# Two of eight Toeplitz blocks' vectors made inside attention, with a block load, a table load and an addition moved

## The reference, cut to what matters

```python
for layer in range(DEPTH):                     # DEPTH = 2
    if layer % 2 == 0:                         # layer 0: attention over the last 128 positions, with sinks
        mp, kp_new, vp_new = swa_prompt(rmsnorm(xp, norm_mix[layer]), *attn)
        ms, ks_new, vs_new = swa_sample(rmsnorm(xs, norm_mix[layer]), cache_k[a], cache_v[a], *attn)
    else:                                      # layer 1: h_l = A h_(l-1) + B u_l, y = Re(C h) + D u
        mp, rp_new, ip_new = s5_mix(rmsnorm(xp, norm_mix[layer]), h0, h0, *ssm)
        ms, rs_new, is_new = s5_mix(rmsnorm(xs, norm_mix[layer]), state_re, state_im, *ssm)
    xp = xp + mp
    xs = xs + ms
    xp = xp + hier_moe(rmsnorm(xp, norm_ffn[layer]), *moe_w)
    xs = xs + hier_moe(rmsnorm(xs, norm_ffn[layer]), *moe_w)
y_prompt, y_sample = rmsnorm(xp, norm_final), rmsnorm(xs, norm_final)

# what the SSM's constants are (s5_mix)
abar = exp(delta * (a_re + 1j * a_im))         # one complex number per group and state
bbar = (abar - 1) / a * b                      # "B-bar"; its factor (abar - 1) / a is CF in the kernel
```

## Time and profile before

| | us |
|---|---|
| median of three runs | 926.05 |
| lowest, highest | 925.84, 927.51 |
| the profiled execution's own time | 925.76 |
| its span in the profile | 923.8 |

### The profile page before, as it was taken

How to read it: one execution, slowest core, us unless ns; L and a number is a source line. 1 busy time by engine, 2 the same in 40 slices (tenths; PEclk the granted TensorE clock), 3 DMA queues, 4 the chain that set the end, 5 groups by cost and what they waited for, 6 DMA issues and landing times.

```text
span 923.8 us, 12813 instructions
## 1 busy us (share of the span) xinstructions
PE 768.5 (83%) x4895; PEld 481.0 (52%) x4895; DVE 405.7 (44%) x1001; ACT 259.9 (28%) x554; POOL 151.3 (16%) x233
## 2 busy tenths in 40 slices
PE   3899977999899898999733689799999888999730
PEld 2344445868545695555423567544345487555410
DVE  3378695867588370111128677301112162211118
ACT  6020034635111202322213355310014311322113
POOL 1020003000779001332110201000000001333110
PEclk9999996979999889999976899899999979999885
DMA  9462135000532898999869787780131296999946
GB/s 341 145 201 101 51 112 221 2 0 2 200 117 114 290 411 303 409 411 402 351 201 309 198 209 174 212 313 0 49 133 46 70 396 245 405 409 408 396 156 226
DMA packets 75381, 201.81 MB, mean 218 GB/s; under 512 B 14872, under 2 KB 29592, under 8 KB 74264
## 3 DMA queue, kind: packets, MB, share of 16 engines
q1 hardware_dynamic: 58360, 161.77, 48.7%
q0 software_dynamic: 9696, 19.75, 6.1%
q10 hardware_dynamic: 7264, 19.46, 5.8%
HBM read 171.64 MB, written 39.39 MB: 228 GB/s over the span
## 4 chain that ended last, share of the span: by engine, by line
PE 63%; DMA 11%; DVE 11%; ACT 6%; SPq 5%; issue 3%; POOL 0%; PEldq 0%; DVEq 0%; POOLq 0%; PEld 0%; ACTq 0%
PE PSUM L2049 14%; PE PSUM L1852 10%; PE PSUM L1637 8%; PE PSUM L1796 7%; PE PSUM L1873 5%; DMA RING<-in_moe_w_up 3%; PE PSUM L1840 3%; DMA RING<-in_attn_w_qkv 3%; DVE X L1515 2%; SPq L476 2%; PE PSUM L1727 2%; PE PSUM L1999 2%; PE PSUM L1995 2%; DVE XNT L773 2%; PE PSUM L1594 2%
## 5 line engine op out<-in xcount | busy, mean ns | idle before, releaser
L1637 PE MATMUL PSUM<-RING,XNT 128*128 128x512 f32 (+2 forms) x256 | 94.5, 567 | 4.3 <-DMA RING<-in_attn_w_qkv 3.6
L1852 PE MATMUL PSUM<-PH 128*64 128x256 f32 x448 | 85.6, 399 | 8.4 <-DMA PH<-in_moe_w_up 3.9
L671 POOL DMA_INDIRECT PH<-xn_scratch,PH x32 | 32.5, 1017 | 342.4 <-DVEq L1459 247.7
L2049 PE MATMUL PSUM<-PH,XNT 128*128 128x512 f32 (+1 forms) x220 | 88.1, 593 | 0.3 <-PE PSUM L2049 0.3
L1852 PE MATMUL PSUM<-RING,PH 128*64 128x256 f32 x384 | 69.4, 392 | 11.2 <-DMA PH<-in_moe_w_up 6.4
L1594 PE MATMUL PSUM<-ONES,IDENT 128*128 128x128 f32 x348 | 49.8, 314 | 24.1 <-DVEq L1518 23.9
L1490 DVE TENSOR_TENSOR PH<-PH,PSUM 128x128 f32<-128x128 f32 x32 | 9.2, 289 | 136.3 <-ACT PH L976 136.3
L1637 PEld LDWEIGHTS PSUM<-RING,XNT 128*128 128x128 f32 (+1 forms) x256 | 40.4, 177 | 53.9 <-issue 47.7
L1852 PEld LDWEIGHTS PSUM<-PH 128*64 128x64 f32 x448 | 51.6, 144 | 27.0 <-issue 11.9
L1796 PE MATMUL PSUM<-RING,PH 128*128 128x512 f32 (+1 forms) x160 | 62.6, 593 | 0.0
L1594 PEld LDWEIGHTS PSUM<-ONES,IDENT 128*128 128x128 f32 x348 | 48.8, 229 | 24.5 <-DVEq L1518 24.0
(11 more groups left out here) (378 smaller groups left out, 1366.7 us busy)
## 6 DMA issues: line engine op xcount, KB each, us to landing
PH<-in_moe_w_gate SPq DMA_DIRECT2D x28, 512.0 KB, 10.9
PH<-in_moe_w_up SPq DMA_DIRECT2D x28, 512.0 KB, 13.2
RING<-in_moe_w_gate SPq DMA_DIRECT2D x24, 512.0 KB, 11.5
RING<-in_moe_w_up SPq DMA_DIRECT2D x24, 512.0 KB, 16.0
RING<-in_moe_w_down SPq DMA_DIRECT2D x24, 512.0 KB, 16.3
PH<-in_moe_w_down SPq DMA_DIRECT2D x24, 512.0 KB, 14.8
RING<-in_attn_w_qkv SPq DMA_DIRECT2D x4, 1536.0 KB, 18.3
XNT<-in_moe_w_gate SPq DMA_DIRECT2D x12, 512.0 KB, 16.6
```

The source lines that it names most:

```text
L671: pool.indirect_dma_start(out=XG[:, i % 2, :], out_offset=None, in_=xn_d[layer], in_offset=bass.IndirectOffsetOnAxis(ap=IDX[:, i:i + 1], a ...
L1637: last = te.matmul(PSUM[lo:hi, b0 + col // 512, col % 512:col % 512 + n], XT[:, c, t * P:t * P + r], RING[:, c // 2, (c % 2) * QKV + col:( ...
L1852: last = te.matmul(PSUM[m * 64:(m + 1) * 64, 2 + i % 2, 0:2 * FF], XGT[:, i % 2, c, m * 64:(m + 1) * 64], gu[:, :, c, :], start=(c == 0), ...
L2049: last = te.matmul(PSUM[p0:p0 + r, 2 * (i % 2) + w, :], XT[:, c, t * P:t * P + r], slot(SLOT[q])[:, (2 * (c % 3) + w) * 512:(2 * (c % 3) + ...
```

## The change

- DVE: blocks 6 and 7 are no longer made behind tile 3. They are made in attention by a new function `v_half`, half a block at a time (six operations on 128 x 288 elements), at the end of the turns i = 1 to 4 of DVE's loop; block 6 in turns 1 and 2, block 7 in turns 3 and 4. They lie in a buffer of their own, VH, so that block 7's first half waits until block 6 is written out.
- POOL: B-bar is made in two halves, in place (twelve operations on 128 x 256 elements).
- ACT: an exponential of one element stands before the end of phase 1.
- DVE: X + BO stands ahead of the wait for the product.
- SP: block 0 is asked for behind the last expert weights, block 1 behind the copies to AL.

```diff
             for k in range(NB):
                 sp.wait_ge(S("v_ready"), k + 1)
-                sp.dma_start(blk_d[k][:, 0:2 * TAPS].rearrange("p (r n) -> p r n", r=2), VQ[:, k % 2]
+                sp.dma_start(blk_d[k][:, 0:2 * TAPS].rearrange("p (r n) -> p r n", r=2), VQ[:, k % 2] if k < 6 else VH
...
             experts(0)
+            block_in(0)
             sp.wait_ge(S("ring_free"), Q_M0 + 28)
             sp.dma_start(INS, in_d).then_inc(S("ins_in"), 16)
...
             rows_back(0)
-            for k in (0, 1):
-                block_in(k)
             for t in tiles(2):
...
-            for k in (2, 3):
+            for k in range(1, 4):
                 block_in(k)
...
-            cf = [bc(CF[:, r, :].unsqueeze(2), [P, GP, CH]) for r in range(2)]
-            pool.tensor_tensor(BT1, cf[0], BBI[:, 0], ALU.mult)
...
+            for g0 in range(0, GP, GP // 2):
+                gs = slice(g0, g0 + GP // 2)
+                cf = [bc(CF[:, r, gs].unsqueeze(2), [P, GP // 2, CH]) for r in range(2)]
...
+            nc.scalar.activation(SS[:, 1, 0:1], EPSC[:, :], ACT.Exp)
             end_phase(act, 1)
...
-                for k in {0: (0, 1), 1: (2, 3), 2: (4, 5), 3: (6, 7), 4: ()}[t]:
+                for k in {0: (0, 1), 1: (2, 3), 2: (4, 5), 3: (), 4: ()}[t]:
                     v_block(k)
             end_phase(dve, 1)
             for b in range(2):
-                dve.wait_ge(S(f"vec_out{b}"), 16 * NB // 2)
+                dve.wait_ge(S(f"vec_out{b}"), 16 * 3)
...
+            def v_half(k, half):
+                g0 = BP * k + 2 * half
+                four = [P, 2, 9, CH]
...
+                if half == 0 and k == 7:
+                    dve.wait_ge(S("vec_out0"), 16 * NB // 2)
+                ve.tensor_tensor(t1, c_[0], a_[0], ALU.mult)
+                ch(ve.tensor_tensor(t2, c_[1], a_[1], ALU.mult))
+                ch(ve.tensor_tensor(o[0], t1, t2, ALU.add))
...
+                if half:
+                    dve.sem_inc(S("v_ready"), 1)
...
                 if i:
                     out_scale(i - 1)
+                if 1 <= i <= 4:
+                    v_half(6 + (i - 1) // 2, (i - 1) % 2)
...
                 r = ROWS[t]
+                ch(ve.tensor_tensor(X[0:r, t, :], X[0:r, t, :], BO[0:r, :], ALU.add))
                 dve.wait_ge(S("wo_done"), t + 1)
                 b0 = 4 + 2 * (t % 2)
-                ch(ve.tensor_tensor(X[0:r, t, :], X[0:r, t, :], BO[0:r, :], ALU.add))
```

More of the change, by code:

```diff
@@ L184, in build @@
         BBI = XN[:, 4, :].rearrange("p (r g c) -> p r g c", r=2, g=GP)
-        BBQ = CT
-        BT1, BT2 = [QO.rearrange("p b n -> p (b n)")[:, 256 + 512 * j:768 + 512 * j].rearrange("p (g c) -> p g c", g=GP) for j in range(2)]
-        PWRQ = QO.rearrange("p b n -> p (b n)")[:, 1280:1280 + 2 * 9 * GP].rearrange("p (r k g) -> p r k g", r=2, k=9)
+        BBQ = BBI
+        QOF = QO.rearrange("p b n -> p (b n)")
+        BT = [QOF[:, 256 + 256 * j:512 + 256 * j].rearrange("p (g c) -> p g c", g=GP // 2) for j in range(4)]
+        VH = XNF[:, 2 * D:2 * D + 2 * TAPS].rearrange("p (r n) -> p r n", r=2)
+        VS1, VS2 = [XNF[:, 2 * D + (4 + j) * TAPS // 2:2 * D + (5 + j) * TAPS // 2] for j in range(2)]
+        assert 2 * D + 3 * TAPS <= 4 * D
+        PWRQ = QOF[:, 1280:1280 + 2 * 9 * GP].rearrange("p (r k g) -> p r k g", r=2, k=9)
         assert a.at <= PH_F
@@ L610, in _ @@
             pool.tensor_copy(PWRQ[:, :, 8, :], PW[:, :, 8, :])
-            cf = [bc(CF[:, r, :].unsqueeze(2), [P, GP, CH]) for r in range(2)]
-            pool.tensor_tensor(BT1, cf[0], BBI[:, 0], ALU.mult)
[L613 to L617, removed]
+            for g0 in range(0, GP, GP // 2):
+                gs = slice(g0, g0 + GP // 2)
+                cf = [bc(CF[:, r, gs].unsqueeze(2), [P, GP // 2, CH]) for r in range(2)]
+                b = [BBI[:, r, gs, :] for r in range(2)]
+                pool.tensor_tensor(BT[0], cf[0], b[0], ALU.mult)
+                pool.tensor_tensor(BT[1], cf[1], b[1], ALU.mult)
+                pool.tensor_tensor(BT[2], cf[0], b[1], ALU.mult)
+                ch(pool.tensor_tensor(BT[3], cf[1], b[0], ALU.mult))
+                pool.tensor_tensor(b[0], BT[0], BT[1], ALU.subtract)
+                ch(pool.tensor_tensor(b[1], BT[2], BT[3], ALU.add))
             pool.sem_inc(S("bb_ready"), 1)
@@ L1245, in sink_of @@
                 return SINK[:, 4 * h:4 * h + 4].rearrange("p (g w) -> p w g", w=2)
+            def v_half(k, half):
+                g0 = BP * k + 2 * half
+                four = [P, 2, 9, CH]
+                a_ = [bc(PW[:, r, :, g0:g0 + 2].rearrange("p k g -> p g k").unsqueeze(3), four) for r in range(2)]
+                c_ = [bc(CT[:, r, g0:g0 + 2, :].unsqueeze(2), four) for r in range(2)]
+                t1, t2 = [v.rearrange("p (g s c) -> p g s c", g=2, s=9) for v in (VS1, VS2)]
+                o = [VH[:, r, half * TAPS // 2:(half + 1) * TAPS // 2].rearrange("p (g s c) -> p g s c", g=2, s=9)
+                     for r in range(2)]
+                if half == 0 and k == 7:
[3 more added lines that the diff above has]
+                ch(ve.tensor_tensor(o[0], t1, t2, ALU.add))
+                ve.tensor_tensor(t1, c_[1], a_[0], ALU.mult)
+                ch(ve.tensor_tensor(t2, c_[0], a_[1], ALU.mult))
+                ch(ve.tensor_tensor(o[1], t1, t2, ALU.subtract))
+                if half:
+                    dve.sem_inc(S("v_ready"), 1)
             def scale_mask(i):
@@ L1340, in _ @@
                     out_scale(i - 1)
+                if 1 <= i <= 4:
+                    v_half(6 + (i - 1) // 2, (i - 1) % 2)
+                if i == 9:
+                    dve.wait_ge(S("vec_out1"), 16 * NB // 2)
             out_scale(NU - 1)
```

## The result

| | before | after |
|---|---|---|
| median of 20 runs each | 927.75 | 933.81 |
| lowest | 923.04 | 928.18 |
| profiled execution | 925.76 | 933.24 |
| its span | 923.8 | 931.4 |

The ratio is 1.0082, 95% interval 1.0059 to 1.0104: slower by some 7.6 us (the interval stands for 5.5 to 9.6, and the medians differ by 6.1), where +3.3 was forecast and 933.0 was the upper end of the range. The two profiles differ by 7.6 us as well. An execution now and then is some per cent longer as a whole; the ratios leave those out, and so does the table of the experiments (the profile of e7). The next table cuts both at eleven events that every kernel here has; the stretches are differences of starts in the timelines.

The account below looks back on a forecast made before the run. Bounds taken: DVE at phase 1's end, unit chains then PE in attention, the product in W_O, the DMA queue between experts and SSM. 5.3 - 1.2 - 0.8 = +3.3 gave 929.4 us, range 925.2 to 933.0.

Parts of the forecast that it names:

- End of phase 1: End of the QKV projection: DVE starts the sample tile earlier, PE no longer waits, table load moves; together -0.9 us.
- bias: W_O: the last tile's BO addition moves into DVE's idle time ahead of it, -1.2 us.
- halves up to the sample unit: Attention's first units: four halves take 11.3 us, DVE has room for 5.1; +6.2, attention ends 5.3 later.
- AL: Ahead of the SSM: AL's copies follow the rows directly, in at about 508.2 rather than 512.4, -4.2 us.
- the wait for the Toeplitz copies: SSM: the copies queue behind three blocks; first outputs start at 523.6 rather than 525.74, -2.1 us.
- rival 1: SSM: the queue does not hold the Toeplitz copies, -4.2 comes in full, 926.0 us; chance 0.17.
- the half clock at the first outputs: SSM: PE idles before the first outputs, then runs them at the half clock; +1.3 us, ends 0 and +2.6.
- Block 0: Behind the last expert weights: its 3.5 us load fits free DMA time, nothing is late; 0, at the worst +1.
- Rival 4: The edits don't take: block 0's place frees too late, runs into INS and last rows' scatter, +1 to +3.5; chance 0.03.
- Everything behind moves along with it: Behind the terms summed: later stages only shift along with the sum of +3.3 us.
- rival 3: Attention: PE's clock stays at 0.50 until the halves are over, +3, 932.4 us; chance 0.17.
- Rival 2: DVE's turns 1 to 4 in attention: the halves hide, 923.1 us, with rival 1 as well 919.7; chance 0.13.

Follow-up runs that it names:

- e7: Changed kernel without halves, blocks' places as before, small edits kept, three blocks' vectors behind tile 2 and one behind tile 3: 0.9978 of the kernel before.
- e4: Changed kernel with block 0 alone moved back, behind the expert rows; blocks 1 to 3 stay behind the copies to AL: 1.0032 of the kernel before.
- e6: Changed kernel with block 1 alone moved back, behind the rows; block 0 stays behind the last expert weights: 1.0049 of the kernel before.
- e3: Changed kernel with halves and blocks' places both undone; early table load, bias ahead of the wait and B-bar in halves stay: 0.9958 of the kernel before.
- e2: Changed kernel with blocks 0 and 1 behind the rows again, 2 and 3 behind the copies to AL; halves stay: 1.0015 of the kernel before.
- e5: Changed kernel with table load, bias and blocks' places undone; the halves alone, with B-bar in place: 1.0070 of the kernel before.
- e10: Changed kernel with filler matmuls on PE, 36 ahead of the first outputs and 16 ahead of the third: 1.0117 of the kernel before.
- e13: Changed kernel with shorter filler on PE, 17 matmuls ahead of the first outputs and 7 ahead of the third: 1.0051 of the kernel before.

## Why the prediction missed

- **The side was right, the size not**: +3.3 forecast, about +7.6 measured, and 933.81 against a range up to 933.0.
- **End of phase 1, bias, halves up to the sample unit, AL, the wait for the Toeplitz copies**: right, each within 0.5 us, as told above (-1.2 and 1.18, 5.3 and 5.8, 4.2 and 4.25, 2.1 and 1.8). The Toeplitz copies did wait behind the three blocks, and e4 against e6 (15.62 and 12.91 us) prices the third block at 2.7 us: rival 1 falls. This agrees with the ring order that the Trainium skill states in "DMA: Bandwidth & Descriptors", section on queues, rings and completion order. Two figures on the way don't come out of their own terms: AL's 508.2 (502.4 + 2 x 3.3 - 1.5 is 507.5) and the bound of 2.6 us for the half clock at the first outputs (4.7 us at 1.22 to 0.67 is 3.9 more). Measured were 508.3, when the later start of the rows is taken off, and 1.5 to 2.6.
- **Block 0**: this term failed: "nothing is late: 0, at the worst +1". I counted the free share of the DMA engines (0.41 busy) and took 3.5 us for the load, which landed after 16.9; and I checked when INS is asked for, but not the expert scatters on POOL's queue, whose landing frees the buffers that DVE writes and releases the rows. It cost 2.2 in the profile and 2 in six profiles of six. By time, e4, the changed kernel without this term, is 3.0 us over the kernel before, near the +3.3, but its interval is 3 us wide to either side. Rival 4 had the scatter in it, at 0.03 and for another reason (a place that comes free too late).
- **"Everything behind moves along with it"**: this failed too, by 4.4 us, 3.6 of it from the second to the fourth outputs. e3, with neither the halves nor the new places, shows it as well, so it is not shown to be theirs, and its cause stays open; what failed is that I took one execution for the stage's length: from the second to the fourth outputs it had 20.36 us, where e2, e3 and e5, with the blocks at the same places, had 21.97 to 24.36.
- **The clock in attention**: rival 3 was half right. The clock did stay low until the halves were over (0.60 from 154 to 173.4). But the profile got 3.5 us back in the sample units, whose half clock I had left in the sum as it was: "it can't be made good later" was wrong. In e10 and e5 the clock was low behind the halves as well, and more was lost than came back. By time, the halves cost 5.3 us (e2 against e3), near the forecast's 6.2, with intervals too wide to tell that from the 0.5 to 2.6 us that five profiles of six show in attention.
- **Rival 2** (the halves hide) falls: DVE masks right behind each half, and it has 18.35 of 19.40 us busy.
- **Open**: why the changed kernel is 11.5 us over e3 when the parts alone are 5.3 and 2.9 over it. The intervals allow that they add up. Open too: what the small edits gave beyond the bias.

## What to carry to other kernels

A load put into an idle stretch of the DMA engines has to be checked against every queue that uses them, indirect scatters included, and against whoever waits for those to land; where a compute step hides a load anyway, as the norm did with one block, nothing is won by asking earlier. Work put into a loop that has 5 us of room for 11 us of it delays what stands behind it (here by 6.9 us at the sample unit), though a later stretch may give part back; that it is better put where its engine idles, behind tile 2, is likely, but e7 alone doesn't show it. And one profile gives a stage's length only as well as the stage repeats: a stretch with waits and half-clock spells needs several executions before it goes into a sum.

## What the runs showed of the hardware

Attention, the same instructions in the same order, took 101.34 to 103.37 us in five profiles (after, e2, e4, e6, e13) and 112.60 in a sixth (e10), and the difference goes with where and how long TensorE ran at the half clock (1.2 GHz), even with PE busy throughout (27 of 27 us at 0.50). I had taken the half clock as a matter of idle waits alone. And one 1.5 MB load, asked for beside the last experts, landed 16.9 us later, and with it a scatter issued 6.9 us behind it took 9.3 us to land and INS 11.1; without it, the same scatter took 6.9 and INS 6.6. In six profiles with that load and seven without, the two groups don't overlap.
